# A two-block transformer kernel on one core: softplus of the first attention in two fp32r parts, layer norm on VectorE, and other orders of work

## What is computed

```python
x = x + 0.5 * swiglu(rmsnorm(x, ff1_norm), w_gate, w_up, w_down)     # ff1, d_ff 2816
h = rmsnorm(x, mix_norm); proj = h @ w_in                            # a_in, q, k, v, gates
u, v = split(gelu(a_in)); v = layernorm(v, ln_g, ln_b)               # per group of 256, 4 groups
s_mix = einsum('gts,bnsgc->bntgc', w_masked, v) + b_s; y_a = u * s_mix
# stick-breaking attention, 16 heads of 64, for queries t and keys s < t
z = q @ k.T / 8
log_keep = where(causal, -softplus(z), 0)
log_w = log_sigmoid(z) + cumsum(log_keep, reverse) - log_keep
y_b = where(causal, exp(log_w), 0) @ v
merged = g_a * (y_a @ w_a) + g_b * (y_b @ w_b); x = x + merged @ w_out
x = x + 0.5 * swiglu(rmsnorm(x, ff2_norm), ...); x = rmsnorm(x, final_norm)
```

## Time and profile before

| what | value |
|---|---|
| median of 3 runs | 1244.16 us (1243.75 to 1244.47) |
| the profiled execution's own time | 1244.19 us |
| its span, first to last instruction | 1242.4 us |
| mean granted TensorE clock | 0.998 |
| TensorE busy | 1224.5 us (99%) |
| VectorE, ScalarE, POOL busy | 816.7, 625.8, 171.1 us |

### The profile page before, as it was taken

The page is one execution under the profiler, slowest core; times in us unless marked ns, Lnnn a source line. Parts: engine busy times, 40 slices in busy tenths (PEclk is TensorE's granted clock), DMA queues, the critical chain, the costliest instruction groups (busy, mean ns, idle before and its releaser), DMA issues.

```text
span 1242.4 us, 17592 instructions
## 1 busy us (share of the span) xinstructions
PE 1224.5 (99%) x6847; PEld 1047.5 (84%) x6847; DVE 816.7 (66%) x1229; ACT 625.8 (50%) x965; POOL 171.1 (14%) x224
## 2 busy tenths in 40 slices
PE   8999999999999999999999999999999999999997
PEld 7888888888878888888878988888888888888886
DVE  6766666344676667766676766875765576876764
ACT  6544436554644347444446566544446365744443
POOL 1222210122030003222102310000000541000000
PEclk9999999999999999999999999999999999999999
DMA  7755566533847455655665435865562555675540
GB/s 248 246 180 184 189 201 186 185 105 94 295 132 224 146 170 174 201 192 188 195 195 153 137 119 186 268 189 189 186 200 76 171 164 163 195 252 189 191 147 35
DMA packets 174907, 221.74 MB, mean 178 GB/s; under 512 B 9084, under 2 KB 103896, under 8 KB 174824
## 3 DMA queue, kind: packets, MB, share of 16 engines
q1 hardware_dynamic: 173496, 216.86, 55.2%
q0 software_dynamic: 880, 2.70, 0.8%
q10 hardware_dynamic: 448, 1.05, 0.2%
HBM read 219.52 MB, written 1.06 MB: 178 GB/s over the span
## 4 chain that ended last, share of the span: by engine, by line
PE 88%; DVE 6%; ACT 4%; issue 1%; DMA 0%; POOL 0%; ACTq 0%; DVEq 0%; POOLq 0%
PE bank L1431 48%; PE bank L1517 22%; PE bank L1524 11%; DVE w_lo L961 3%; PE bank L1454 1%; PE bank L1688 1%; ACT w_hi L618 1%; PE bank L1671 1%; PE bank L1661 1%; DVE xt L996 1%; ACT xt L656 1%; DVE x L1073 1%; DVE a_uv L1317 1%; PE bank L1648 1%; PE bank L1646 1%
## 5 line engine op out<-in xcount | busy, mean ns | idle before, releaser
L961 DVE TENSOR_TENSOR w_lo<-raw,w_hi 128x1024 fp32r<-128x1024 f32 (+1 forms) x448 | 499.2, 1137 | 234.3 <-ACT w_hi L618 234.0
L618 ACT ACTIVATE w_hi<-raw 128x1024 fp32r<-128x1024 f32 (+1 forms) x448 | 420.5, 972 | 278.3 <-PE bank L1524 146.6
L1517 PE MATMUL bank<-xt,w_hi 128*128 128x512 f32 x1216 | 316.6, 392 | 0.4 <-ACT w_hi L618 0.4
L1517 PEld LDWEIGHTS bank<-xt,w_hi 128*128 128x128 f32 x1216 | 215.8, 189 | 35.1 <-ACT w_hi L618 0.6
L1524 PEld LDWEIGHTS bank<-xt,w_lo 128*128 128x128 f32 x1216 | 170.6, 190 | 15.3
L1524 PE MATMUL bank<-xt,w_lo 128*128 128x256 f32 x1216 | 175.1, 282 | 0.0
L1431 PE MATMUL bank<-w_hi,xt 128*128 128x512 f32 x512 | 160.1, 394 | 1.9 <-DVE w_lo L961 1.1
L1431 PE MATMUL bank<-w_hi,yt_lo 128*128 128x512 f32 x336 | 132.2, 394 | 0.0
L1431 PE MATMUL bank<-w_hi,yt_hi 128*128 128x512 f32 x336 | 130.9, 390 | 0.0
L1431 PE MATMUL bank<-w_lo,yt_hi 128*128 128x512 f32 x336 | 130.9, 390 | 0.0
L1431 PE MATMUL bank<-xt,w_hi 128*128 128x256 f32 x640 | 115.9, 283 | 0.0
(11 more groups left out here) (198 smaller groups left out, 1202.1 us busy)
## 6 DMA issues: line engine op xcount, KB each, us to landing
raw<-in_w_up SPq DMA_DIRECT2D x64, 512.0 KB, 4.2
raw<-in_w_down SPq DMA_DIRECT2D x64, 512.0 KB, 4.4
raw<-in_w_in SPq DMA_DIRECT2D x56, 512.0 KB, 4.5
raw<-in_ff_w_gate SPq DMA_DIRECT2D x88, 256.0 KB, 2.9
raw<-in_ff_w_up SPq DMA_DIRECT2D x88, 256.0 KB, 3.2
raw<-in_ff_w_down SPq DMA_DIRECT2D x88, 256.0 KB, 4.4
raw<-in_moba_w_qkv SPq DMA_DIRECT2D x24, 512.0 KB, 4.2
raw<-in_w_o SPq DMA_DIRECT2D x16, 512.0 KB, 3.6
```

The source lines that it names most:

```text
L618: act.activation(w_hi[:, c % RING, 0:w], raw[:, c % RAW, 0:w], ACT.Copy).then_inc(s["hi_ready"], 1)
L961: dve.tensor_tensor(w_lo[:, c % RING, 0:w], raw[:, c % RAW, 0:w], w_hi[:, c % RING, 0:w].bitcast(F32), ALU.subtract).then_inc(s["lo_ready" ...
L1517: ins = pe.matmul(up_banks(m)[q][:], w_h[:, k % 2, q * P:(q + 1) * P], flat(xt[:, k, :, :]), start=k == 0, stop=False, skip_group_check=True)
```

## The change

1. The softplus of the first attention is split, after the mask, into an fp32r high part (`tensor_copy` on VectorE) and a low part (subtraction on VectorE), in buffers made from `ht_hi` and `ht_lo`. `middle` multiplies both by fp32r copies of the triangle over all 384 columns at once and by fp32r `nones` over 128 columns: four fp32r matmuls for a head in place of three plain fp32 ones.
2. VectorE's cycle becomes `second_part(pr+1)`, `halves(pr+1)` (the two parts), `q_evac`, `lo(c+2)`, `y_part`, `k_evac`, `lo(c+3)`. `halves(0)` stands ahead of `lo(b+11)`, `halves(7)` ahead of `lo(b+26)`.
3. Layer norm: two `scalar_tensor_tensor` passes of eight instructions on VectorE; POOL's four instructions go.
4. `ffn_end`: the low parts of the next phase's units 2 and 3 move behind `add_half(0)` and `add_half(1)`.
5. The start: the gain load moves from ScalarE's queue to the head of POOL's, and ScalarE and VectorE take each quarter of x transposed and then one weight unit, four times.

```diff
+        sp_hi, sp_lo = (v.rearrange("p a b -> p (a b)")[:, 0:6 * P].rearrange("p (h n) -> p h n", h=2)
+                        for v in (ht_hi[:], ht_lo[:]))
 ...
+            pool.dma_start(gain_rows[0:8, :], ff1_norm.rearrange("a (k p) -> (a k) p", p=P)).then_inc(s["gain_in"], 16)
             pool.memset(eps[:], EPS).then_inc(s["zero_done"], 1)
 ...
+            const(pool.tensor_copy(ntri_r[:], ntri[:]))
+            const(pool.tensor_copy(nones_r[:], nones[:]))
 ...
-            pool.wait_ge(s["blk1_in"], 32)
-            for tok in range(TOK):
-                v = a_uv[:, tok, 0:D]
-                pool.wait_ge(s["ln_done2"], GROUPS * (tok + 1))
-                pool.tensor_tensor(v, v, ln_rows[0], ALU.mult).then_inc(s["lng_done"], 1)
-                pool.wait_ge(s["lng_done"], tok + 1)
-                pool.tensor_tensor(v, v, ln_rows[1], ALU.add).then_inc(s["v_ln"], 1)
 ...
-            act.dma_start(gain_rows[0:8, :], ff1_norm.rearrange("a (k p) -> (a k) p", p=P))\
-                .then_inc(s["gain_in"], 16)
 ...
-            turned("turn_ff1", 0, [(xt_hi, 0)])
-            hi(0)
-            turned("turn_ff1", 1, [(xt_hi, 0)])
-            for u in range(1, AHEAD):
+            for u in range(AHEAD):
+                turned("turn_ff1", u // 2, [(xt_hi, 0)], (u % 2,))
                 hi(u)
 ...
-                    for u in range(10 if m < n - 1 else 8, 12):
+                    for u in (10, 11) if m < n - 1 else (8, 9):
                         lo(c + u)
 ...
             def ffn_end(phase, scale, between):
                 b = at(phase, "units") + dict(PHASES)[phase]["units"]
                 add_half(phase, scale, 0, b - 3)
+                lo(b + 2)
                 between()
                 add_half(phase, scale, 1, b - 1)
+                lo(b + 3)
 ...
+                def halves(pr):
+                    if kind != "stick":
+                        return
+                    for h in range(2):
+                        n = 2 * pr + h + 1
+                        if pr:
+                            dve.wait_ge(s["r_ready"], hp + 2 * pr)
+                        dve.wait_ge(s["spm_done"], at(phase, "spm_done") + n)
+                        dve.tensor_copy(sp_hi[:, h, :], work[1][:, h, 0:3 * P]).then_inc(s["sp_hi"], 1)
+                        dve.wait_ge(s["sp_hi"], at(phase, "sp_hi") + n)
+                        dve.tensor_tensor(sp_lo[:, h, :], work[1][:, h, 0:3 * P], sp_hi[:, h, :].bitcast(F32),
+                                          ALU.subtract).then_inc(s["sp_lo"], 1)
 ...
                     first_part(pr + 1)
-                    if kind == "stick":
-                        lo(c + 2)
-                        q_evac(c, e)
-                    elif pr:
+                    if kind != "stick" and pr:
                         y_part(pr - 1)
                     second_part(pr + 1)
-                    if kind != "stick":
-                        q_evac(c, e)
-                        lo(c + 2)
-                    elif pr:
+                    halves(pr + 1)
+                    q_evac(c, e)
+                    lo(c + 2)
+                    if kind == "stick" and pr:
                         y_part(pr - 1)
                     k_evac(c, e)
                     lo(c + 3)
 ...
                 second_part(0)
+                halves(0)
                 if kind != "fox":
                     lo(b + 11)
 ...
                     second_part(PAIRS - 1)
                     y_part(PAIRS - 3)
+                    halves(PAIRS - 1)
                     lo(b + 26)
 ...
+            dve.wait_ge(s["blk1_in"], 32)
             for n in range(TOK * GROUPS):
-                dve.tensor_scalar(v, v, bn2[:, n, 0:1], ln_rstd[:, n:n + 1], ALU.subtract, ALU.mult)
+                dve.scalar_tensor_tensor(v, v, bn2[:, n, 0:1], ln_rows[0][:, cols], ALU.subtract, ALU.mult)
+            for n in range(TOK * GROUPS):
+                dve.wait_ge(s["lng_done"], n + 1)
+                dve.scalar_tensor_tensor(v, v, ln_rstd[:, n:n + 1], ln_rows[1][:, cols], ALU.mult, ALU.add)
 ...
-                            pe.matmul(z[:, 0:S], ntri[:], sp[:, h, 0:S], start=False, stop=True, ...)
-                            pe.matmul(z[:, P:S], nones[:], sp[:, h, S:3 * P], start=False, stop=True, ...)
-                            ins = pe.matmul(z[:, S:3 * P], ntri[:], sp[:, h, S:3 * P], start=False, ...)
+                            pe.wait_ge(s["sp_lo"], at(phase, "sp_lo") + 2 * pr + h + 1)
+                            for sp in (sp_hi, sp_lo):
+                                pe.matmul(z[:, 0:3 * P], ntri_r[:], sp[:, h, :], start=False, stop=True, ...)
+                            for sp in (sp_hi, sp_lo):
+                                ins = pe.matmul(z[:, P:S], nones_r[:], sp[:, h, S:3 * P], start=False, ...)
```

More of the change, by code:

```diff
@@ L75 @@
 STICK = {"abs_done": HEADS, "exp_done": HEADS, "ln_done": HEADS, "sp_done": HEADS, "spm_done": HEADS,
+         "sp_hi": HEADS, "sp_lo": HEADS,
          "wm_done": HEADS}
@@ L177, in two_blocks @@
         nones = sb("nones", [P, P])
+        ntri_r = sb("ntri_r", [P, P], F32R)
+        nones_r = sb("nones_r", [P, P], F32R)
         gain_rows = sb("gain_rows", [P, P])
@@ L645, in inverse_root, with turned @@
                 act.activation(dst[:], rms[:], ACT.Exp, scale=-0.5).then_inc(s["rstd_done"], 1)
-            def turned(phase, half, sets):
+            def turned(phase, half, sets, parts=(0, 1)):
                 banks = turn_banks(phase, half)
-                for b in range(2):
+                for b in parts:
                     act.wait_ge(s["tr_ready"], at(phase, "tr_ready") + 2 * half + b + 1)
@@ L1273, in _ @@
             dve.wait_ge(s["gain_cols"], 1)
[L1274 to L1277, removed]
+            for u in range(AHEAD):
+                turned("turn_ff1", u // 2, [(xt_lo, xt_hi, 0)], (u % 2,))
                 lo(u)
@@ L1313, in _ @@
             dve.wait_ge(s["lnr_done"], 1)
+            dve.wait_ge(s["blk1_in"], 32)
             for n in range(TOK * GROUPS):
                 tok, g = divmod(n, GROUPS)
-                v = a_uv[:, tok, g * GD:(g + 1) * GD]
-                dve.tensor_scalar(v, v, bn2[:, n, 0:1], ln_rstd[:, n:n + 1], ALU.subtract, ALU.mult)\
-                    .then_inc(s["ln_done2"], 1)
+                cols = slice(g * GD, (g + 1) * GD)
+                v = a_uv[:, tok, cols]
+                dve.scalar_tensor_tensor(v, v, bn2[:, n, 0:1], ln_rows[0][:, cols], ALU.subtract, ALU.mult)\
+                    .then_inc(s["lng_done"], 1)
+            for n in range(TOK * GROUPS):
+                tok, g = divmod(n, GROUPS)
+                cols = slice(g * GD, (g + 1) * GD)
+                v = a_uv[:, tok, cols]
+                dve.wait_ge(s["lng_done"], n + 1)
+                dve.scalar_tensor_tensor(v, v, ln_rstd[:, n:n + 1], ln_rows[1][:, cols], ALU.mult, ALU.add)\
+                    .then_inc(s["v_ln"], 1)
             dve.wait_ge(s["gate_in"], 64)
@@ L1657, in middle @@
                         if kind == "stick":
-                            pe.wait_ge(s["spm_done"], at(phase, "spm_done") + 2 * pr + h + 1)
-                            z, sp = z_bank(e, h), work[1]
-                            pe.matmul(z[:, 0:S], ntri[:], sp[:, h, 0:S], start=False, stop=True,
-                                      skip_group_check=True)
-                            pe.matmul(z[:, P:S], nones[:], sp[:, h, S:3 * P], start=False, stop=True,
-                                      skip_group_check=True)
-                            ins = pe.matmul(z[:, S:3 * P], ntri[:], sp[:, h, S:3 * P], start=False, stop=True,
-                                            skip_group_check=True)
+                            pe.wait_ge(s["sp_lo"], at(phase, "sp_lo") + 2 * pr + h + 1)
+                            z = z_bank(e, h)
+                            for sp in (sp_hi, sp_lo):
+                                pe.matmul(z[:, 0:3 * P], ntri_r[:], sp[:, h, :], start=False, stop=True,
+                                          skip_group_check=True)
+                            for sp in (sp_hi, sp_lo):
+                                ins = pe.matmul(z[:, P:S], nones_r[:], sp[:, h, S:3 * P], start=False, stop=True,
+                                                skip_group_check=True)
                         else:
@@ L1875, in _ @@
                 tok, g = divmod(n, GROUPS)
-                pe.wait_ge(s["v_ln"], tok + 1)
+                pe.wait_ge(s["v_ln"], GROUPS * (tok + 1))
                 ins = pe.matmul(bank[4 + 2 * tok + g // 2][:, (g % 2) * GD:(g % 2 + 1) * GD], wst[:, g, :],
```

4 lines of the change are left out of this document (2 added, 2 removed).

## The result

The changed kernel takes 1237.65 us (median of 6 runs, 1237.25 to 1238.52) beside 1244.85 us for the kernel before on the same chips. The ratio is 0.9943, with an interval of 0.9931 to 0.9956: faster by 0.57%, 7.1 us by the ratio. The forecast was 1235.0 us, 9.2 less than before, with a range of 1231.5 to 1240.0.

A forecast was written before the change was run, and what follows sets the result against it. The prediction took TensorE as the bound, busy 1224.5 of 1242.4 us. Its terms, 4.8 + 3.4 - 0.9 - 2.5 + 2.6 + 1.3 + 0.5 = 9.2 us, took 1244.19 to 1235.0 us, range 1231.5 to 1240.0.

The forecast's parts named there:

- `halves(0)`: Ahead of the first attention's pair 1: TensorE stalls for unit 11, queued behind these parts; 2.5 us lost, bounds 2.0 to 3.5.
- the start: Kernel start: the gain load's move costs nothing, the new order saves 0.5 us; bounds 1.3 saved and 1.0 lost.
- triangle: First attention's `middle`: fp32r matmuls save 0.30 us a head, 4.8 us over 16 heads; bounds 1.3 and 6.4.
- wait ahead of `middle`: First attention's cycles: `second_part` starts at once, so TensorE's idle time before `middle` goes; 3.4 us saved.
- FFN ends: Ends of ff1 and ff2: `add_half` no longer queues behind two low parts; 2.6 us saved, bounds 2.0 and 3.0.
- layer norm: Layer norm: with POOL idle, the gates' low parts come in time; 1.3 us saved, bounds 0.8 and 1.5.
- k late: First attention's `scores`: k's evacuation comes late by 0.15 us in each of six cycles; 0.9 us lost.
- third rival: VectorE becomes the attention's bound, its new operations and POOL's masks blocking one another; 1239 to 1245 us, say 1240; chance 0.13.
- rival on the slower side: Attention: the same blocking at 1.35 us an operation, a cycle of 12.7 us against 9.82; about 1259 us; chance 0.04.

The follow-up runs named there:

- e5: The changed kernel with the old three plain fp32 matmuls a head and no fp32r parts on VectorE, the new order kept: 0.9938 of the kernel before, 1236.92 us.
- e2: The changed kernel with `halves(0)` moved behind `lo(b+11)`: 0.9916 of the kernel before, 1233.41 us.
- e10: The changed kernel with the edits of e1, e2 and e4 together: 0.9888 of the kernel before, 1230.72 us.
- e4: The changed kernel with `lo(c+2)` behind `k_evac` and a wait of the scores for an old Exp: 0.9932 of the kernel before, 1235.88 us.
- e6: The changed kernel with the low parts of the next phase's units 2 and 3 ahead of `add_half` again: 0.9959 of the kernel before, 1238.92 us.
- e7: The changed kernel with the old layer norm, POOL's four instructions included: 0.9955 of the kernel before, 1239.26 us.
- e1: The changed kernel with the gain load back at the head of ScalarE's queue, ahead of x: 0.9934 of the kernel before, 1235.96 us.
- e8: The changed kernel with POOL doing eight multiplications nobody reads from the layer norm's reciprocal on: 1.0026 of the kernel before, 1247.76 us.
- e9: The changed kernel with `lo(c+2)` and `q_evac` ahead of softplus as before, the parts right behind softplus: 1.0063 of the kernel before, 1252.03 us.
- e3: The changed kernel with `lo(b+11)` between the two heads of `halves(0)`: 0.9932 of the kernel before, 1235.51 us.
- e11: As e10, but with the gain load behind x on ScalarE's queue: 0.9895 of the kernel before, 1231.44 us.

## Why the prediction was right, point by point

The direction and the mechanisms held, and the time lies in the range; the sum of 9.2 us was 2.5 us too large in the profiled execution (6.7). What came out worse than forecast (`halves(0)`, the start, k) is 3.9 us in all, what came out better (triangle, wait ahead of `middle`, FFN ends, layer norm) 1.2; so a third of the misses cancelled by luck, and the rest is the 2.5 to 2.7 us by which the sum is off.

| term of the sum | forecast | measured | from |
|---|---|---|---|
| triangle in fp32r | -4.8 | -5.3 | 8 x (1.85 - 1.19) |
| wait ahead of `middle` | -3.4 | -3.6 | 71.79 - 68.16, e5 |
| k late | +0.9 | +1.7 | 65.25 - 63.57, e2 and e10; e4 |
| `halves(0)` | +2.5 | +4.4 | 2.8 stall, 1.6 clock; e2 |
| FFN ends | -2.6 | -2.7 | table above, e6 |
| layer norm | -1.3 | -1.7 | table above, e7 |
| start | -0.5 | +0.7 | row of roots; e1, e10 |

The measured terms make 6.5 us, and the x transposes after ff2 are 6.4 earlier; the last 0.3 of the 6.7 come behind TensorE's last matmul.

Two steps were wrong. *The start*: "They ended 1.22 us before x was there, so this costs nothing". I priced the load's move by POOL's time to issue it, bounded from a row, and gave its landing no price at all. It could be used 5.5 us after the issue began, 1.6 us after TensorE wanted it, and the saved half microsecond, which e10 shows to be real (22.37 to 21.83), became a loss of 0.7. My own bound for a loss (1.0) rested on the clock, not on this. *`halves(0)`*: "Bounds: 2.0 to 3.5". The stall was 2.8, inside; but in the profiled execution the stall took the clock with it and the step came to 4.4, outside. The prediction did weigh the clock at the start and nowhere else.

The smaller sizes: the first narrow fp32r matmul of a pair takes 0.06 us to the start of the next with the same weights, where I took 0.11; that is the lower bound I had named. The second, ahead of a change of weights, takes 0.11, so that the pair is 0.17 (237.00 to 237.17) against my 0.22. The copy costs 0.35 us alone (230.05) and 0.53 to 0.58 where POOL's mask overlaps it, against my 0.42, twice a cycle: some 0.3 us a cycle, enough by size for k's lateness beyond the forecast (0.8 us over six cycles). It looks as if the third rival's mechanism, operations of VectorE and POOL that hold each other up, was at work in small, at 0.2 us for each copy; but no run takes the masks away, and the one copy without a mask beside it is that of `halves(0)`, so this is not shown.

What the rivals had right: VectorE did become the next bound (e4), by 0.2 us a cycle and 0.7 in the second. The rival on the slower side stayed out, but e8 and e9 show that both of its ingredients are real: the blocking at 1.3 us an instruction, and a cycle of 11.0 us as soon as the parts come late. In e9 TensorE waits for the parts, but whether blocking or only the order makes them late there, no run separates.

## What to carry to other kernels

A wait put into an in-order queue costs what stands behind it: the fp32r split was level with plain fp32 until one weight unit was taken out from behind `halves(0)` and one from ahead of `k_evac`. Price a stall of the multiplying engine of some 2 us twice, once for its length and once for a clock that may fall with it. When a load changes queues, price its landing and not only its issue, and keep a small load that the first instructions need ahead of the large ones.

## What the runs showed of the hardware that was not expected

Behind a stall of TensorE of 2.8 us, and behind one of 1.9 us in e3, the granted clock stood at 0.50 (1.2 GHz) until well into the next microseconds (to about 235.7 in the changed kernel), with matmuls of 256 columns 0.21 us apart in place of 0.12. The length of a stall doesn't settle whether that happens. In the kernel before, TensorE stood still for 1.54 us ahead of the x transposes at the end of ff1 and the clock stayed at 1.00; in e9 it stayed so behind waits of 1.53 and 1.52 us (270.65 and 281.68) and fell at 294.9, behind one of 1.52 (292.70). And among the changed kernel's six executions, with mean clocks of 0.997 to 1.000, at least one had no fall behind the same queue. A 4 KB load issued right behind that of x could be used only 4.9 (e11) to 5.5 us after it began to issue; ahead of x it took 3.2 us at most (e1). And fp32r at 128 columns ran at 0.06 us with the weights unchanged, half of the 0.12 for 256 columns, where no row of the kernel before had shown it.
